# A mixture-of-experts decoder block: down weights by column halves, and a new order of the last steps

## The chip, the cores and the metric

The kernel runs on one core of one Trainium2 chip. The metric is device time in microseconds (us): how long one execution of the whole program takes, weights read from the chip's memory and the result written back to it. The time before is the median of three runs.

## What is computed

The reference is one layer of a decoder for 256 tokens of width 1024 in float32: two kinds of attention side by side, merged by gates (the head of the kernel), then a mixture of 32 experts, and a last norm. The part that the change touches, shortened:

```python
# moe_ffn: each token goes to its 4 best experts of 32, weighted by a softmax
g = xb @ w_gate[e] + b_gate[e]
u = xb @ w_up[e] + b_up[e]
g = jnp.minimum(g, 7.0); u = jnp.clip(u, -7.0, 7.0)
h = (u + 1.0) * g * jax.nn.sigmoid(1.702 * g)
out = h @ w_down[e] + b_down[e]          # summed per token with its gate
x = x + y
return x * rsqrt(mean(x * x, axis=-1) + 1e-5) * norm_final_g   # rms_norm
```

## The kernel before

The experts are worked off two at a time: 16 pairs, each with 64 places for tokens per expert. In `expert_iteration` two pairs make one iteration; the first and the last iteration are written out, the others are a hardware loop. One matmul's left operand holds the 64 tokens of one expert, and the two experts of a pair run side by side in the two halves of the columns of TensorE's array. In float32 one product appears as two matmul instructions in the trace.

The weights of a pair come in 12 loads of 2048 KB (numbers 0 to 3 gate, 4 to 7 up, 8 to 11 down) into a ring of 12 slots that holds just one pair. SyncE (SP) issues them: in the loop two neighbouring loads by one issue (`load_unit`, 4096 KB), in the first and last pairs one by one (`load_half`), and the very last in two pieces (`load_last`). Each issue waits on `load_used`, which TensorE raises when it has done with a slot of the pair before. TensorE waits on `slot_loaded` or `unit_loaded` before it uses one.

The down weights (loads 8 to 11) are laid out by rows: load 8+m holds two of the eight chunks of 128 rows for each of the two experts, over all 1024 columns. `down(w, m, half, c)` adds a chunk's product to one of two accumulator banks, the left 512 columns (`half` 0) or the right. So both halves of the result are complete only when the last load has been used. Between load 8 and load 9 stands `transpose_hidden(1)`, which turns the second half of the hidden layer. When the left half is done (`down_done`) ScalarE copies it to `o_s`, and after the last product the right half (L648). Then TensorE scatters: four products of 512 columns (`scatter(a, half)`, L1486) add the pair's result to `y`, which stays in four accumulator banks over all pairs, one for each block `a` of 128 tokens and each half. In one pair of two, `gather_next` (L1359) then fetches the tokens of the next pair.

After the last pair every engine asks in `rounds_after_first` (L329, L330) whether an expert had more than 64 tokens; it reads one number from memory and branches. Here no second round is run. The end then runs like this. VectorE adds `y` to `x` in four steps of 512 columns (L1068: left and right of block 0, then of block 1). ScalarE loads the table for roots (L654), sums the squares of each step (L658), and takes the root for each block (L663); VectorE prepares a term of it (`half_bias`, L1074) and takes the reciprocal (L1084). Block 0 is multiplied by the norm's weights on GpSimd (L480) and by the reciprocal on ScalarE (L669), block 1 by both on VectorE (L1090). The norm's weights, `gfin`, are read by one load of 512 KB, the same 4 KB for each of 128 partitions, that SP issues when the last pair's hidden layer has been transposed (L443). SP issues the four stores of 256 KB, in the order left and right of block 0, left and right of block 1 (L448), and waits until all have landed.

## Time and profile before

| what | value |
|---|---|
| median of 3 runs | 1138.95 us |
| lowest and highest run | 1138.13 and 1140.11 us |
| the profiled execution's own time | 1142.86 us |
| its span, first to last instruction | 1141.0 us |
| TensorE matmul busy | 1067.4 us, 94% |
| VectorE, ScalarE, GpSimd busy | 210.5, 133.4, 7.9 us |
| mean granted TensorE clock | 0.989 |
| moved by DMA | 438.16 MB, mean 384 GB/s |

The profile is of one execution; its times are counted from the start of the span. "Busy" of TensorE is modelled: matmuls overlap, so one instruction's duration is longer than its share of the time. The granted clock is 1.00 for 2.4 GHz and 0.50 for 1.2 GHz. A row of a timeline names the line of the kernel and the operation, output before input, the count, and in brackets how long the engine stood idle before it and what it waited for. PE is TensorE's matmuls, DVE VectorE, ACT ScalarE; SPq and ACTq are the queues of instructions of SP and ScalarE.

### The profile page before, as it was taken

The numbers are of one execution on the slowest core, as the hardware profiler recorded it, in microseconds if no ns is written. First come the engines' busy times: TensorE is split into PE (matmuls) and PEld (weight loads), VectorE is DVE, ScalarE is ACT, GpSimd is POOL, SyncE is SP. The second block draws the span as 40 slices with busy tenths as digits, with TensorE's granted clock in tenths as the row PEclk, the third lists the DMA queues.
The fourth block names the chain that finished last, engine by engine and source line by source line (L and its number), as shares of the span: only waits on it lengthen the run. The fifth ranks groups of instructions, "written<-read, shape, count | busy, mean of one in ns | idle before, by whom it ended". The sixth has DMA issues, their size and how long they took to land.

```text
span 1141.0 us, 11734 instructions
## 1 busy us (share of the span) xinstructions
PE 1067.4 (94%) x4990; PEld 493.5 (43%) x4990; DVE 210.5 (18%) x508; ACT 133.4 (12%) x227; POOL 7.9 (1%) x17
## 2 busy tenths in 40 slices
PE   8999999989999999999999897989798979998986
PEld 6686888643443434344324332433243324332321
DVE  3132143122211121202020202020202020202021
ACT  1112260111001001000100000001000100010002
POOL 1000000000000000000000000000000000000000
PEclk9999999989999999999999999999999999999998
DMA  9972354589999999999999999999999999999994
GB/s 345 427 304 92 148 219 168 204 345 428 426 434 429 433 430 430 433 431 433 431 432 431 433 430 434 430 434 430 434 430 434 428 435 427 437 421 430 426 428 187
DMA packets 25646, 438.16 MB, mean 384 GB/s; under 512 B 4880, under 2 KB 6160, under 8 KB 8464
## 3 DMA queue, kind: packets, MB, share of 16 engines
q1 hardware_dynamic: 25472, 437.67, 90.5%
q8 instruction: 22, 0.36, 0.1%
q10 hardware_dynamic: 144, 0.07, 0.0%
q14 instruction: 8, 0.07, 0.0%
HBM read 436.28 MB, written 1.05 MB: 383 GB/s over the span
## 4 chain that ended last, share of the span: by engine, by line
PE 70%; DMA 26%; another core or an unknown queue 2%; ACT 1%; DVE 1%; issue 0%; SPq 0%; ACTq 0%; DVEq 0%
PE ps L1433 26%; DMA ring<-in_experts 25%; PE ps L1477 15%; PE ps L1123 9%; PE ps L1359 4%; PE ps L1486 3%; PE ps L1265 2%; PE ps L1114 2%; PE ps L1313 1%; PE ps L1310 1%; PE ps L1142 1%; PE ps L1466 1%; PE ps L1368 1%; ACT region_va L640 1%; PE ps L1378 0%
## 5 line engine op out<-in xcount | busy, mean ns | idle before, releaser
L1433 PE MATMUL ps<-ring,xT 128*64 128x512 f32 x2048 | 453.1, 596 | 28.6 <-DMA ring<-in_experts 28.5
L1433 PEld LDWEIGHTS ps<-ring,xT 128*64 128x64 f32 x2048 | 142.7, 137 | 313.9 <-issue 277.2
L1477 PE MATMUL ps<-ring,region_va 128*64 128x512 f32 x1024 | 233.4, 606 | 28.0 <-DMA ring<-in_experts 18.8
L1477 PEld LDWEIGHTS ps<-ring,region_va 128*64 128x64 f32 x1024 | 73.6, 139 | 166.2 <-issue 129.5
L1123 PE MATMUL ps<-ring 128*128 128x256 f32 x448 | 98.6, 380 | 0.3 <-DVE ring L694 0.3
L1123 PEld LDWEIGHTS ps<-ring 128*128 128x128 f32 x448 | 84.5, 190 | 12.9 <-issue 1.5
L1019 DVE TENSOR_SCALAR g<-ps 128x1024 f32<-128x1024 f32 x16 | 19.6, 1225 | 350.6 <-PE ps L1433 350.6
L1359 PEld LDWEIGHTS ps<-sel,x 128*128 128x128 f32 x480 | 55.4, 192 | 9.5 <-issue 9.5
L1486 PE MATMUL ps<-g,g_T 128*128 128x512 f32 x128 | 59.2, 605 | 0.0
L967 DVE TENSOR_TENSOR xT<-ps,g_ffn 128x512 f32<-128x512 f32 x30 | 20.8, 692 | 197.7 <-PE ps L1359 197.7
L1359 PE MATMUL ps<-sel,x 128*128 128x128 f32 x480 | 56.7, 276 | 0.0
L1041 DVE TENSOR_SCALAR region_va<-ps 128x512 f32<-128x512 f32 x32 | 22.1, 692 | 176.9 <-PE ps L1433 176.9
L634 ACT ACTIVATE region_va<-g 128x1024 f32<-128x1024 f32 x16 | 16.9, 1057 | 318.2 <-DVE g L1019 318.2
L640 ACT COPY region_va<-ps 128x512 f32<-128x512 f32 x32 | 18.8, 586 | 243.6 <-PE ps L1466 243.6
L1486 PEld LDWEIGHTS ps<-g,g_T 128*128 128x128 f32 x128 | 22.9, 189 | 36.0 <-issue 27.5
L648 ACT COPY g<-ps 128x512 f32<-128x512 f32 x32 | 18.8, 587 | 162.6 <-PE ps L1477 162.6
L1114 PE MATMUL ps<-ring 128*128 128x512 f32 x64 | 27.8, 592 | 0.0
L1466 PEld LDWEIGHTS ps<-ident,g 128*128 128x128 f32 x128 | 13.8, 141 | 20.4 <-issue 20.4
L1044 DVE SCALAR_TENSOR_TENSOR g<-region_va,g 128x512 f32<-128x512 f32 x32 | 22.1, 692 | 1.1
L1142 PE MATMUL ps<-ring 128*128 128x256 f32 x64 | 16.4, 420 | 5.0 <-DVE ring L679 5.0
L1466 PE MATMUL ps<-ident,g 128*128 128x128 f32 x128 | 20.3, 281 | 0.0
L1368 PE MATMUL ps<-bias,oh 96*128 96x512 bf16 x64 | 19.7, 389 | 0.0
(200 smaller groups left out, 443.5 us busy)
## 6 DMA issues: line engine op xcount, KB each, us to landing
ring<-in_experts SPq DMA_DIRECT2D x72, 4096.0 KB, 47.5
ring<-in_experts SPq DMA_DIRECT2D x47, 2048.0 KB, 18.4
ring<-in_head SPq DMA_DIRECT2D x13, 2048.0 KB, 16.6
ring<-in_first SPq DMA_DIRECT2D x7, 384.0 KB, 6.1
ring<-in_experts SPq DMA_DIRECT2D x2, 1024.0 KB, 49.5
x<-in_x SPq DMA_DIRECT2D x2, 512.0 KB, 25.0
out<-x SPq DMA_DIRECT2D x4, 256.0 KB, 2.5
ring<-in_norm_final_g SPq DMA_DIRECT2D x1, 512.0 KB, 13.1
```

What stands on the lines that cost most here:

```text
L640: nc.scalar.copy(hTm[:, 4 * b:4 * b + 4, :], bank(second + b).rearrange("p (c s) -> p c s", c=4)).then_inc(hT_ready, 1)
L1041: steps.step(nc.vector.tensor_scalar(u_s[:, cols], bank(second + half), LIMIT, -LIMIT, ALU.min, ALU.max))
L1114: last = mm(bank(b + a), hT[:, c, a * P:(a + 1) * P], w[:, c, :], start=c == 0, stop=c == KC - 1)
L1123: last = mm(bank(b + j // 2)[:, (j % 2) * T:(j % 2 + 1) * T], wj, h, start=c == 0, stop=c == KC - 1)
L1142: last = mm(bank(4 + j)[:, 0:T], w_first[:, c, j * P:(j + 1) * P], hg[:, c, :], start=c == 0, stop=c == KC - 1)
L1265: last = mm(bank(first_bank + j // 2)[:, (j % 2) * T:(j % 2 + 1) * T], w[:, c, j * P:(j + 1) * P], heads[:, c, :], start=c == 0, stop=c == 3)
L1359: last = mm(bank(banks + c // 4)[:, (c % 4) * P:(c % 4 + 1) * P], x3[:, a, c * P:(c + 1) * P], s_sel[:, a, :], start=a == 0, stop=a == NT - 1)
L1368: mm(bank(banks + half), oh[n % 2][0:3 * E, :], bias3[0:3 * E, which, half * W512:(half + 1) * W512], start=True, stop=False, skip_group_c ...
L1433: last = mm(bank(banks + half)[rows, :], xT[:, 2 * m + c, rows], w[:, c, k, half * W512:(half + 1) * W512], start=False, stop=m == 3 and c ...
L1466: last = nc.tensor.transpose(bank(second + b)[:, (c % 4) * P:(c % 4 + 1) * P], g_s[:, c * P:(c + 1) * P], ident)
L1477: last = mm(bank(first + half)[rows, :], hTm[:, 2 * m + c, rows], w[:, c, k, half * W512:(half + 1) * W512], start=m == 0 and c == 0, stop ...
L1486: mm(bank(Y_B + 2 * a + half), g_T[:, a * P:(a + 1) * P], o_s[:, half * W512:(half + 1) * W512], start=False, stop=True, skip_group_check= ...
```

## The change

The down weights are laid out by column halves on the host: loads 8 and 9 hold the left 512 columns of all eight chunks (four chunks each), loads 10 and 11 the right 512 columns. `down(m, chunks)` follows that, and the scatter of the left half (both blocks of tokens) moves between loads 10 and 11; the scatter of the right half stays at the end. ScalarE's copy of the left half waits for load 9's products and that of the right half for load 11's. `transpose_hidden(1)` moves into the middle of load 8. The last load is split at three quarters instead of half.

The norm's weights come at the start as a small load of 4 KB, one column per chunk (`g_fin`). In the last pair TensorE spreads them over all partitions by eight products of 128 columns into two free accumulator banks (`spread_gain`), between loads 9 and 10. The 512 KB load and GpSimd's part are gone. The root table is loaded in the last pair before the left copy. At the end the left halves of both blocks come first: VectorE multiplies them by the norm's weights, ScalarE by the reciprocal; the right halves are multiplied by both on VectorE. SP issues three stores, ScalarE's queue the fourth (left half of block 1). The number of weight bytes, of down products and of scatters is unchanged.

The diff, cut to its core (most removed lines can be seen in the functions above):

```diff
+LAST_COL = 3 * SLOT_COLS // 4
...
-        gfin = whole(SLOT_OF[0])[:, 0:D]
-        xg = whole(SLOT_OF[0])[:, D:2 * D]
+        xg = whole(SLOT_OF[0])[:, 0:D].rearrange("p (a n) -> p a n", a=NT)
...
+        GAIN_B = pair_bank(PAIRS_PER_ITER)
...
+                sp_.dma_start(g_fin[:, :], norm_final_g).then_inc(ld_gfin, 16)
...
-                for c, loaded in enumerate((last_rows, unit_loaded[UNITS - 1])):
-                    cols = slice(c * (SLOT_COLS // 2), (c + 1) * (SLOT_COLS // 2))
-                    from_cols = slice((2 + c) * (SLOT_COLS // 2), (3 + c) * (SLOT_COLS // 2))
-                    sp_.dma_start(whole(SLOT_OF[p])[:, cols], experts_v[row][:, from_cols]).then_inc(loaded, 16)
+                for lo, hi, loaded in ((0, LAST_COL, last_rows), (LAST_COL, SLOT_COLS, unit_loaded[UNITS - 1])):
+                    sp_.dma_start(whole(SLOT_OF[p])[:, lo:hi], experts_v[row][:, SLOT_COLS + lo:SLOT_COLS + hi]
+                                  ).then_inc(loaded, 16)
...
-            rounds = rounds_after_first(sp_, load_iteration)
-            sp_.wait_ge(ht_done, rounds * (2 * PAIRS))
-            sp_.dma_start(gfin, norm_final_g.partition_broadcast(P)).then_inc(ld_gfin, 16)
-            for a in range(NT):
-                for half in range(2):
-                    cols = slice(half * W512, (half + 1) * W512)
-                    sp_.wait_ge((fin_done0, fin_done)[a], half + 1)
-                    sp_.dma_start(out_d[a * P:(a + 1) * P, cols], x3[:, a, cols]).then_inc(stored, 16)
+            rounds_after_first(sp_, load_iteration)
+            for done, a, half in ((fin_right, 0, 1), (fin_left, 0, 0), (fin_right, 1, 1)):
+                cols = slice(half * W512, (half + 1) * W512)
+                sp_.wait_ge(done, a + 1)
+                sp_.dma_start(out_d[a * P:(a + 1) * P, cols], x3[:, a, cols]).then_inc(stored, 16)
...
-            pool.wait_ge(ld_gfin, 16)
-            for half in range(2):
-                cols = slice(half * W512, (half + 1) * W512)
-                pool.wait_ge(y_added, half + 1)
-                nc.gpsimd.tensor_tensor(xg[:, cols], x3[:, 0, cols], gfin[:, cols], ALU.mult).then_inc(fin_g, 1)
...
+            def load_root_table():
+                nc.scalar.activation(table_junk, ones_row[:, 0:2], ACT.Sqrt)
...
+                    if closing and q == PAIRS_PER_ITER - 1:
+                        load_root_table()
                     for b in range(2):
-                        if b == 0:
-                            act.wait_ge(down_done, n + 1)
-                        else:
-                            act.wait_ge(load_used, it * LOADS_PER_ITER + LOADS_PER_PAIR * (q + 2))
+                        act.wait_ge(load_used, it * LOADS_PER_ITER + LOADS_PER_PAIR * (q + 1) + 10 + 2 * b)
                         nc.scalar.copy(o_s[:, b * W512:(b + 1) * W512], bank(first + b)).then_inc(o_ready, 1)
-            with act.Fori(0, ITERS) as i:
+            with act.Fori(0, ITERS - 1) as i:
                 expert_iteration(i, i)
-            rounds_after_first(act, expert_iteration)
-            nc.scalar.activation(table_junk, ones_row[:, 0:2], ACT.Sqrt)
+            expert_iteration(ITERS - 1, ITERS - 1, closing=True)
+            rounds_after_first(act, expert_iteration, closing=load_root_table)
+            def final_squares(a, half):
+                act.wait_ge(y_added, 2 * half + a + 1)
+                nc.scalar.activation(fin_junk[:, (2 * a + half) * W512:(2 * a + half + 1) * W512],
+                                     x3[:, a, half * W512:(half + 1) * W512], ACT.Square,
+                                     accum_out=fin_ssq[:, 2 * a + half:2 * a + half + 1]).then_inc(ssq1_ready, 1)
             for a in range(NT):
-                for half in range(2):
...
+                final_squares(a, 0)
+            for a in range(NT):
+                final_squares(a, 1)
+                act.wait_ge(ssq1_ready, NT + a + 1)
                 act.wait_ge(fin_bias_ready, a + 1)
                 nc.scalar.activation(std[:, a:a + 1], fin_ssq[:, 2 * a + 1:2 * a + 2], ACT.Sqrt, scale=1.0 / D,
                                      bias=fin_bias[:, a:a + 1]).then_inc(fin_std, 1)
...
+            for a in range(NT):
+                act.wait_ge(fin_g, a + 1)
+                act.wait_ge(rstd_ready, a + 1)
+                nc.scalar.activation(x3[:, a, 0:W512], xg[:, a, :], ACT.Copy,
+                                     scale=rstd[:, a:a + 1]).then_inc(fin_left, 1)
+            act.wait_ge(fin_left, NT)
+            act.dma_start(out_d[P:T, 0:W512], x3[:, 1, 0:W512]).then_inc(stored, 16)
...
-                                        resume=lambda: gathered(PAIRS + 1, pair_bank(1)))
...
+                                        resume=lambda: gathered(PAIRS + 1, pair_bank(1)),
+                                        closing=lambda: dve.wait_ge(gain_spread, 4))
+            def add_experts(a, half):
+                cols = slice(half * W512, (half + 1) * W512)
+                dve.wait_ge(sc_done, rounds * (SC_PER_PAIR * PAIRS) + 2 * half + a)
+                nc.vector.tensor_tensor(x3[:, a, cols], bank(Y_B + 2 * a + half), x3[:, a, cols],
+                                        ALU.add).then_inc(y_added, 1)
...
+            def left_gain(a):
+                dve.wait_ge(y_added, a + 1)
+                nc.vector.tensor_tensor(xg[:, a, :], x3[:, a, 0:W512], bank(GAIN_B), ALU.mult).then_inc(fin_g, 1)
+            add_experts(0, 0)
+            add_experts(1, 0)
+            dve.wait_ge(gain_spread, 2)
+            for a in range(NT):
+                left_gain(a)
+            for a in range(NT):
+                half_bias(a)
+            add_experts(0, 1)
+            add_experts(1, 1)
             for a in range(NT):
                 dve.wait_ge(fin_std, a + 1)
                 nc.vector.reciprocal(rstd[:, a:a + 1], std[:, a:a + 1]).then_inc(rstd_ready, 1)
                 dve.wait_ge(rstd_ready, a + 1)
...
+                nc.vector.scalar_tensor_tensor(out=x3[:, a, W512:D], in0=x3[:, a, W512:D], scalar=rstd[:, a:a + 1],
+                                               in1=bank(GAIN_B + 1), op0=ALU.mult, op1=ALU.mult).then_inc(fin_right, 1)
...
+            def spread_gain():
+                pe.wait_ge(ld_gfin, 16)
+                for c in range(KC):
+                    last = mm(bank(GAIN_B + c // 4)[:, (c % 4) * P:(c % 4 + 1) * P],
+                              g_fin[:, c:c + 1].to_broadcast([P, P]), ident, start=True, stop=True)
+                    if c % 4 == 3:
+                        last.then_inc(gain_spread, 1)
...
+                    def down(m, chunks):
+                        s = SLOT_OF[2 * UNITS - 4 + m]
+                        w = whole(s).rearrange("p (c k n) -> p c k n", c=4, k=2)
+                        half, side = divmod(m, 2)
+                        for c in chunks:
+                            for k in range(2):
+                                rows = slice(k * SLOTS, (k + 1) * SLOTS)
+                                last = mm(bank(first + half)[rows, :], hTm[:, 4 * side + c, rows], w[:, c, k, :],
+                                          start=side == 0 and c == 0, stop=side == 1 and c == 3, skip_group_check=True)
                         return last
...
+                    def scatter(half):
+                        pe.wait_ge(o_ready, n * 2 + half + 1)
+                        for a in range(NT):
+                            mm(bank(Y_B + 2 * a + half), g_T[:, a * P:(a + 1) * P],
+                               o_s[:, half * W512:(half + 1) * W512], start=False, stop=True,
+                               skip_group_check=True).then_inc(sc_done, 1)
+                    loaded(8)
+                    pe.wait_ge(hT_ready, n * 2 + 1)
+                    down(0, (0, 1))
+                    transpose_hidden(1)
+                    down(0, (2, 3)).then_inc(load_used, 1)
+                    loaded(9)
+                    pe.wait_ge(hT_ready, n * 2 + 2)
+                    down(1, range(4)).then_inc(load_used, 1)
                     if last_pair:
-                        down(w, 3, 0, 0)
-                        down(w, 3, 1, 0)
+                        spread_gain()
+                    loaded(10)
+                    down(2, range(4)).then_inc(load_used, 1)
+                    scatter(0)
+                    loaded(11)
+                    if last_pair:
+                        down(3, range(3))
                         pe.wait_ge(unit_loaded[UNITS - 1], (n + 1) * 16)
-                        down(w, 3, 0, 1).then_inc(down_done, 1)
-                        down(w, 3, 1, 1).then_inc(load_used, 1)
+                        down(3, (3,)).then_inc(load_used, 1)
                     else:
...
+                        down(3, range(4)).then_inc(load_used, 1)
+                    scatter(1)
...
+            rounds_after_first(pe, expert_iteration, resume=gather_again, closing=spread_gain)
...
-    for w, name in enumerate(("w_gate", "w_up", "w_down")):
+    for w, name in enumerate(("w_gate", "w_up")):
         out[:, w] = a[name].reshape(PAIRS, 2, 2, 4, P, D).transpose(0, 2, 4, 3, 1, 5)
+    by_half = a["w_down"].reshape(PAIRS, 2, KC, P, 2, W512).transpose(0, 4, 3, 2, 1, 5)
+    out[:, 2] = by_half.reshape(PAIRS, 2, P, 4, 2, D)
...
-    give("norm_final_g", a["norm_final_g"])
+    give("norm_final_g", a["norm_final_g"].reshape(KC, P).T)
```

## Rows read from the trace of the kernel before

**Rows 1.** page, the span in 40 equal slices: DMA share in tenths, GB/s
```profile
DMA  9972354589999999999999999999999999999994
GB/s 345 427 304 92 148 219 168 204 345 428 426 434 429 433 430 430 433 431 433 431 432 431 433 430 434 430 434 430 434 430 434 428 435 427 437 421 430 426 428 187
```

**Rows 2.** page, DMA issues: engine, count, KB each, median us to landing
```profile
ring<-in_experts SPq DMA_DIRECT2D x72, 4096.0 KB, 47.5
ring<-in_experts SPq DMA_DIRECT2D x47, 2048.0 KB, 18.4
...
ring<-in_norm_final_g SPq DMA_DIRECT2D x1, 512.0 KB, 13.1
```

**Rows 3.** windows: us, busy (x) per engine, clock, DMA share, GB/s
```profile
504.33:556.88 52.55, 51.78 (x247) 19.95 (x247) 8.85 (x19) 5.06 (x7) 0.00 (x0) 1.00 1.00 430
```

**Rows 4.** chain of waits, 1110 to 1141 us: start, us, what
```profile
1120.96 8.81 PE ps L1477 x32
...
1129.94 0.48 ACTq L329
```

**Rows 5.** timeline of TensorE, 1094 to 1132 us: start, us, line, operation
```profile
1104.58 3.65 PE L1433 MATMUL ps<-ring,xT 128*64 128x512 f32 x16 [1.24 <-DMA ring<-in_experts]
...
1114.36 3.65 PE L1477 MATMUL ps<-ring,region_va 128*64 128x512 f32 x16 [0.53 <-DMA ring<-in_experts]
1120.96 8.78 PE L1477 MATMUL ps<-ring,region_va 128*64 128x512 f32 x32 [2.95 <-DMA ring<-in_experts]
1129.68 2.84 PE L1486 MATMUL ps<-g,g_T 128*128 128x512 f32 x6
```

**Rows 6.** windows of the low clock (columns as in rows 3)
```profile
1122.00:1125.00 3.00, 3.00 (x10) 0.75 (x8) 0.00 (x0) 0.00 (x0) 0.00 (x0) 0.51 0.27 112
```

**Rows 7.** issues of loads 9 and 10, then of load 11, landings; queues 1118 to 1119
```profile
L393 SPq DMA_DIRECT2D ring<-in_experts x2: 434/2343/4252, 1063.0 to 1067.3; - x2
...
DMA to landing us min/median/max: 51.3/52.5/53.6
...
L407 SPq DMA_DIRECT2D ring<-in_experts x2: 4249/7905/11561, 1069.1 to 1080.7; - x2
...
DMA to landing us min/median/max: 45.0/49.5/54.1
...
q8 instruction: 1, 0.02, 6.9%
```

**Rows 8.** timeline of ScalarE, 1110 to 1141 us
```profile
1113.87 0.59 ACT L640 COPY region_va<-ps 128x512 f32<-128x512 f32 x1 [4.42 <-PE ps L1466]
...
1130.89 1.28 ACT L654 ACT_TABLE_LOAD   x1 [0.51 <-issue]
...
1132.29 0.61 ACT L658 ACTIVATE region_va<-x 128x512 bf16<-128x512 f32 x1
...
1135.22 0.29 ACT L663 ACTIVATE small<-small 128x1 f32<-128x1 f32 x1
1135.42 1.32 ACT L669 ACTIVATE x<-ring,small 128x512 f32<-128x512 f32 x2
```

**Rows 9.** timeline of VectorE, 1128 to 1141 us
```profile
1130.84 0.69 DVE L1068 TENSOR_TENSOR x<-ps,x 128x512 f32<-128x512 f32 x1 [21.14 <-PE ps L1486]
...
1135.98 0.16 DVE L1084 RECIPROCAL small<-small 128x1 f32<-128x1 f32 x1 [1.13 <-ACT small L663]
1136.18 1.42 DVE L1090 SCALAR_TENSOR_TENSOR x<-x,small,ring 128x512 f32<-128x512 f32 x2
```

**Rows 10.** issues of the stores on SP; the load on ScalarE's queue with its landing
```profile
L448 SPq DMA_DIRECT2D out<-x x4: 348/439/777, 1136.2 to 1138.1; - x4
...
ident<-in_const ACTq DMA_DIRECT2D x1, 64.0 KB, 4.0
```

**Rows 11.** timeline of TensorE, whole pairs in the middle
```profile
542.37 10.52 PE L1477 MATMUL ps<-ring,region_va 128*64 128x512 f32 x48
...
646.18 3.84 PE L1359 MATMUL ps<-sel,x 128*128 128x128 f32 x32
```

76 lines of the change are left out of this document (10 added, 66 removed).

## Prediction

> **What bounds the kernel now.** I read the page's slices first [rows 1]: from the tenth slice (of 28.5 us each) to the last but one the DMA engines are full and move about 430 GB/s. The issue table [rows 2] gives the expert weights: 72 x 4096 + 47 x 2048 KB and the last slot in two halves of 1024, together 402.7 MB, so 25.17 MB for each of the 16 pairs of experts. At 430 GB/s one pair takes 58.5 us. A pair whose TensorE never waits takes 52.55 us [rows 3] (the window between equal points of two neighbouring pairs, 51.78 us of it busy). The middle of the kernel is therefore bound by the weight stream, with about 6 us of TensorE slack in each pair, and only what stands behind the last weights can move the end.
>
> So I followed the chain of waits [rows 4] and TensorE's timeline [rows 5] over the last 25 us. The last pair's down weights come in four loads, 8 to 11. Load 9 is multiplied from 1114.36 to 1118.0; then TensorE stands still for 2.9 us until load 10 lands at 1120.9, runs the 32 matmul instructions of loads 10 and 11 in 8.81 us to 1129.77, and goes on with the four scatters. From there the chain is ScalarE's: copy of the right half, the check for more rounds, a table load of 1.28 us, squares, roots, then VectorE's last two products and the stores [rows 8 to 10]. From 1129.77 to the end of the span, 1141.0, are 11.23 us.
>
> Two oddities in this stretch are accidents of timing that the change meets. First, the granted clock falls to 0.5 (1.2 GHz) after the standstill: the window 1122 to 1125 shows a mean of 0.51 [rows 6], TensorE having done nothing from 1118.0 to 1120.9. The 32 instructions at full clock would take 3.65 us for 16 [rows 5] and 3.43 us for each further 16 (10.52 less 3.65, halved [rows 11]), so 7.1 us; the low clock cost 1.7 us. Second, load 10 is late: load 9 was issued at 1063.0 and took 51.3 us, load 10 at 1067.3 and 53.6 us [rows 7]: landings at 1114.3 and 1120.9, 6.6 us apart for 2048 KB, where the rate gives 4.9 us. In between, a packet of 16 KB on the instruction queue took 6.9% of 16 engines for 1 us, so 1.1 us of one engine [rows 7].
>
> **The change, part by part.** TensorE's end. Before, all four 512-column scatters stand behind load 11. After, loads 8 and 9 hold the left half of the down weights and 10 and 11 the right, so the left half is complete at 1118.0 and ScalarE, idle since 1114.5 [rows 8], copies it then. While TensorE waits for load 10 it spreads the norm's weights: 8 products of 128 columns, 16 instructions. The nearest rows are the gather's 32 instructions in 3.84 us [rows 11], so 1.9 us. It lies in the 2.9 us of standstill and costs nothing; without that cover it would cost 1.9. Then come load 10 (16 instructions, 3.43), the two left scatters (4 instructions, 6 take 2.84 with 0.17 of drain, so 1.78 for 4 [rows 5]), load 11 (3.43) and 0.17 of drain: 8.8 us. At full clock the last down product ends at 1120.96 + 8.8 = 1129.8, exactly where it ends now: the left scatters have taken the place of the clock loss. I take full clock, because only 1.0 us of standstill is left, and a stop of 1.24 us in this stretch is followed by full speed (3.65 us for 16 instructions [rows 5]). If the clock falls all the same, add 1.7 us.
>
> Load 11's pieces are now 1536 and 512 KB instead of twice 1024. They landed at 1123.2 and 1125.7 (1069.1 + 54.1, 1080.7 + 45.0; the longer time is the first one's [rows 7]); the first moves to about 1124.5, the second stays. TensorE asks for them at 1126.2 and 1128.8: hidden, by 1.7 and 3.1 us. The 512 KB load of the norm's weights goes away. It is issued behind load 11 on the same queue, after the hidden layer's second transposes (ended by 1113.9), and lands 13.1 us later [rows 2], 1.2 us behind the last weights, so I give it nothing; had it gone between the weights, 1.2 us (512 KB at 430 GB/s) would be won. In its place comes one small load among the start's. The nearest issues hold SP for 0.35 to 0.78 us [rows 10], ahead of most of the head's weights; there the DMA engines soon fall to two to five tenths [rows 1], the head is not short of weights, so again nothing, and 0.8 us at worst.
>
> ScalarE's and VectorE's end, counted from t = the last down product. Unchanged: the copy of the right half starts at 0.03 and takes 0.59, and the round check keeps ScalarE until 1.12 (1129.77 to 1130.89 [rows 4, 8]). The table load of 1.28 and its small activation (1130.89 to 1132.29 together, 1.40 us) have moved into ScalarE's idle time before the left copy (1114.5 to 1118.0, cover 3.5 us). Squares of the left half, 0.61 each: 1.12 to 1.73 and to 2.34, the last sum read out at 2.45. VectorE's two small half_bias steps wait for these sums, and the adds of the right half are queued behind them: this is the new wait. The scatter could release the first add at 0.66 + 1.16 = 1.82 (copy end to first scatter to first add, 1129.68 to 1130.84 [rows 5, 9]), but half_bias holds it to 2.65. Adds: to 3.35 and 3.98. First right square 3.42 to 4.03, sum read to 4.12, root 4.15, second square from 4.36, read to 5.06, root 5.10 to 5.39 (steps and distances as in ScalarE's timeline now, where the second root runs 1135.22 to 1135.51 [rows 8]). From the root's start to the reciprocal are 0.76 us (1135.22 to 1135.98 [rows 8, 9]): reciprocals at 4.91 and 5.88, products of one 512-column half each, 0.75, at 5.11 and 6.08, the last to 6.83. ScalarE's two left products (1.32 for two [rows 8]) end at about 6.8 too, and the copy waits for the same reciprocal.
>
> The Trainium skill (ScalarE: Activation LUTs, section What ACT_TABLE_LOAD costs) gives 1283 ns for the load, as the row does, but adds about 1380 ns of drain for every switch of tables, 2.66 us in all. The rows show the first square 0.12 us behind the load's end, and before the load only 0.5 us without an instruction [rows 8]. By the page the removed switch would give back 2.66 us instead of my 1.40, an estimate of 1136.4 us for the median instead of the sum below; rival 4 is the part of it for which the rows leave room.
>
> Stores. Now the fourth of four on SP starts at 1138.1, although VectorE is done at 1137.6, because each keeps SP for 0.35 to 0.78 us, and its landing ends the span, 2.9 us after that start [rows 10]. After, the third on SP and the one on ScalarE's queue both start at about 6.9. With 2.9 us behind them the span ends at t + 9.8, against 11.23 now: 1.4 us less. Two stores of 256 KB landing together add at most 0.6 us (256 KB at 430 GB/s); I take 0.1. The only load on ScalarE's queue took 4.0 us to land [rows 10], 1.1 more than those 2.9: the upper bound.
>
> Each pair in the middle. The scatter of the right half must now wait for its copy: the last product, 0.03 + 0.59 + about 0.1. That is 0.7 to 0.8 us of TensorE standstill a pair where there was none (the first scatter starts as the products end, 1129.68 [rows 5]). It lies in the 6 us of slack. The slots of loads 10 and 11 come free 1.8 us later than now; the stream's queue covers that (the 2048 KB loads, most of them at the stream's start and its end, land 18.4 us after their issue in the median, over 13 of that behind others [rows 2]).
>
> **Sum.** Span 1141.0 + 0.0 (TensorE) - 1.4 + 0.1 (the tail) = 1139.7; with the 1.9 us around it (1142.86 - 1141.0) 1141.6. The median of the runs, 1138.95, lies 3.9 us under the profiled run, so I apply the difference, -1.3 us: 1137.7.
>
> **The rivals.**
> 1. The clock falls in spite of the spread products: +1.7 - 1.3 = +0.4, 1139.4. For it: a standstill of about 1 us is left. Against: the stop of 1.24 us without a fall. The Trainium skill (TensorE: Matmul & The Clock Gate, section Part 1) has the throttled state as the default, released by activity; by that the spread products can help and not harm.
> 2. Load 10 is on time in ordinary runs, which would also explain why these are 3.9 us shorter than the profiled one (1.6 us of lateness and 1.7 us of clock). Then before restarts at 1119.3 and ends its products at 1126.4; after can't start load 10 before the spread ends (1118.0 + 1.9 = 1119.9, then 8.8: 1128.7). TensorE loses 2.3, the tail gives 1.3: +1.0, 1140.0.
> 3. Load 10 is late before and on time after, because the instruction packet falls elsewhere: TensorE ends at 1128.7 instead of 1129.8, together -2.4: 1136.5.
> 4. The tail gives more: if ScalarE's 0.5 us between its last copy and the next instruction [rows 8] belongs to the table load and not to the round check, the squares start 0.5 us earlier; with stores landing a little sooner 2.0 to 2.5 in all: 1136.7.
> 5. Slower: the new wait in each pair makes TensorE the bound. 15 pairs x 0.75 = 11 us if no slack were left, 1149. It decides only once a pair needs more than 58.5 us; 52.55 + 0.75 = 53.3 speaks against it. A part of it is possible at the start of the stream, where the queue is thin.
> 6. The change does not do what it says at the tail: the store on ScalarE's queue lands 1.1 us later and eats most of the gain: -0.2, 1138.8.
>
> **How the numbers follow.** Chances: forecast 0.42, rival 1 0.10, rival 2 0.20, rival 3 0.10, rival 4 0.07, rival 5 0.05, rival 6 0.06. A measurement of this kernel can tell 0.2%, 2.3 us, from no change. Faster by more takes rival 3, part of 4 and the quick edge of the forecast: 0.22. Slower by more takes rival 5 and the slow edges of 1 and 2: 0.12. Within: 0.66. The range goes from rival 3 less 0.6 us of the runs' own spread, 1135.9, to rival 2 plus the same, 1140.6; the likeliest case alone reaches from 1136.6 to 1138.9.
>
> **What would show it.** In the profile after: 16 gain instructions in about 1.9 us right after load 9; no window under full clock behind 1120; the left scatter between loads 10 and 11; the last down product within 0.3 us of 1129.8; no table load behind the last copy; the first right add at about t + 2.7, after the second half_bias; the last store issued near t + 6.9; the span 9.8 to 10.0 us behind t. In the middle the DMA share stays at 1.00 and each pair shows a stop of 0.7 us before its right scatter. The prediction is wrong if load 10 lands at another time, if the clock falls, or if the DMA share sinks anywhere between 250 and 1110 us.

## The result and the profile after

The changed kernel takes 1142.87 us (median of 15 runs, 1141.35 to 1144.84), the kernel before, beside it, 1139.65 us (15 runs, 1138.13 to 1142.17). The ratio is 1.0028, with a 95% interval of 1.002 to 1.0035: 3.2 us slower. A second measurement (e10, below) gave 1142.92 against 1139.79. The forecast was 1137.7 us and the range ended at 1140.6.

The profiled run of the change has a span of 1141.1 us, that of before had 1141.0 us. They look equal, and that is the first thing to see: every run here takes 1.7 to 2.0 us more than its span, so the profiled run of before took 1142.86 us, 3.2 above its own median, and that of the change 1142.87 us, its median.

TensorE's end after the change, from its timeline (start, us, line, operation, [idle before <- what ended it]), to be laid beside [rows 5]:

```profile
1113.20 1.94 PE L1500 MATMUL ps<-ring,region_va 128*64 128x512 f32 x8
1115.51 3.65 PE L1500 MATMUL ps<-ring,region_va 128*64 128x512 f32 x16 [0.38 <-DMA ring<-in_experts]
1119.10 2.05 PE L1410 MATMUL ps<-ident,g_fin 128*128 128x128 f32 x16
1121.08 3.65 PE L1500 MATMUL ps<-ring,region_va 128*64 128x512 f32 x16
1124.66 1.98 PE L1508 MATMUL ps<-g,g_T 128*128 128x512 f32 x4
1126.58 3.65 PE L1500 MATMUL ps<-ring,region_va 128*64 128x512 f32 x16
1130.92 1.98 PE L1508 MATMUL ps<-g,g_T 128*128 128x512 f32 x4 [0.69 <-ACT g L646]
```

Each piece lies where the prediction put it: the spread products (L1410) behind load 9, the left scatter (the first L1508) between loads 10 and 11, and the stop of 0.69 us in which the right scatter waits for ScalarE's copy. But from 1115.51 on TensorE has no wait for a load any more. The standstill of 2.95 us of [rows 5] is gone, and with it every cover: load 10 had landed at 1120.3 (issued at 1064.3, 56.0 us to landing, in the rows of the issues below), and TensorE began it at 1121.08.

```profile
L398 SPq DMA_DIRECT2D ring<-in_experts x5: 432/4242/11586, 1049.6 to 1064.3; - x5
...
DMA to landing us min/median/max: 51.2/52.4/56.0
```

ScalarE's and VectorE's end, the timelines that answer to [rows 8, 9]; the last down product ends at t = 1130.26 and its copy starts 0.02 us later:

```profile
1130.28 0.58 ACT L646 COPY g<-ps 128x512 f32<-128x512 f32 x1 [10.48 <-PE ps L1500]
1131.55 0.63 ACT L656 ACTIVATE region_va<-x 128x512 bf16<-128x512 f32 x1 [0.69 <-issue]
...
1133.74 0.63 ACT L656 ACTIVATE region_va<-x 128x512 bf16<-128x512 f32 x1 [0.86 <-DVE x L1072]
...
1135.63 1.32 ACT L671 ACTIVATE x<-ring,small 128x512 f32<-128x512 f32 x2
1136.98 0.36 ACTq L674 DMA_DIRECT2D out<-x  x1
```
```profile
1132.91 0.15 DVE L1078 TENSOR_SCALAR small<-small 128x1 f32<-128x1 f32 x1 [0.46 <-ACT region_va L656]
1133.01 1.29 DVE L1072 TENSOR_TENSOR x<-ps,x 128x512 f32<-128x512 f32 x2
...
1135.96 0.75 DVE L1099 SCALAR_TENSOR_TENSOR x<-x,small,ps 128x512 f32<-128x512 f32 x1
```

The table load is gone from here, the second half_bias (L1078) holds the right adds to t + 2.75 (forecast 2.65), VectorE's last product ends at t + 6.45 (forecast 6.83). Up to here the tail is as forecast or better. Yet from t to the end of the span are 10.8 us, not 9.8. The rest is stores. SyncE's three issues (line, engine, start and length on its queue) from its timeline:

```profile
1135.80 2.41 SPq L449 DMA_DIRECT2D out<-x  x3
```

The second of them alone takes 1.33 us (from 1136.37), so the third starts at t + 7.5 and not at t + 6.9.

The middle, in the page's 40 slices (GB/s), against [rows 1]:

```profile
GB/s 346 426 301 95 148 210 168 212 331 430 412 436 434 429 431 431 431 433 430 434 430 434 428 435 427 436 427 436 427 436 426 438 426 438 425 428 429 427 428 191
```

The ninth slice (228 to 257 us), in which the stream begins, shows 331 where before has 345; SyncE's run of 12 issues begins 0.9 us later in this profile (243.08 against 242.15), and 0.9 us at 430 GB/s are those 14. The eleventh (285 to 314 us) shows 412 where before has 426. It is the first slice within the stream in which the changed kernel moves clearly less; e10 to e12 below go into it.

### The profile page after: what moved, and what is told of

Read it like the earlier page. It is cut to its first block, busy times and chain, and to the rows that moved or that the text cites. A ratio compares the mean times of both kernels' runs of the same rounds, so it can differ in the third digit from the quotient of the medians.

```text
span 1141.1 us, 11751 instructions
## 1 busy us (share of the span) xinstructions
PE 1076.3 (94%) x5006; PEld 492.2 (43%) x5006; DVE 211.8 (19%) x510; ACT 132.2 (12%) x226; POOL 5.3 (0%) x15
## 3 DMA queue, kind: packets, MB, share of 16 engines
HBM read 435.76 MB, written 1.05 MB: 383 GB/s over the span
## 4 chain that ended last, share of the span: by engine, by line
PE 70%; DMA 26%; ACT 1%; DVE 1%; issue 1%; another core or an unknown queue 1%; SPq 0%; ACTq 0%; DVEq 0%
PE ps L1451 28%; DMA ring<-in_experts 26%; PE ps L1500 13%; PE ps L1132 9%; PE ps L1508 3%; PE ps L1368 3%; PE ps L1274 2%; PE ps L1123 2%; PE ps L1322 1%; PE ps L1319 1%; PE ps L1151 1%; PE ps L1484 1%; PE ps L1377 1%; ACT region_va L639 1%; ACT g L646 1%
## 5 line engine op out<-in xcount | busy, mean ns | idle before, releaser
L1500 PE MATMUL ps<-ring,region_va 128*64 128x512 f32 x1024 | 233.0, 599 | 18.8 <-ACT region_va L639 11.5
L1500 PEld LDWEIGHTS ps<-ring,region_va 128*64 128x64 f32 x1024 | 70.1, 137 | 156.7 <-issue 131.0
L1508 PE MATMUL ps<-g,g_T 128*128 128x512 f32 x128 | 63.5, 618 | 11.0 <-ACT g L646 11.0
L1508 PEld LDWEIGHTS ps<-g,g_T 128*128 128x128 f32 x128 | 21.7, 189 | 53.4 <-issue 28.3
L1484 PEld LDWEIGHTS ps<-ident,g 128*128 128x128 f32 x128 | 14.1, 143 | 21.2 <-issue 21.2
```

What stands on the lines that cost most here:

```text
L1484: last = nc.tensor.transpose(bank(second + b)[:, (c % 4) * P:(c % 4 + 1) * P], g_s[:, c * P:(c + 1) * P], ident)
L1500: last = mm(bank(first + half)[rows, :], hTm[:, 4 * side + c, rows], w[:, c, k, :], start=side == 0 and c == 0, stop=side == 1 and c == 3, ...
L1508: mm(bank(Y_B + 2 * a + half), g_T[:, a * P:(a + 1) * P], o_s[:, half * W512:(half + 1) * W512], start=False, stop=True, skip_group_check= ...
```

## The experiments

An interval of a ratio here is about 0.1% to either side, 1.1 us, so a step of one experiment beside another is known to about that; the profiles tell more exactly where a microsecond lies. All differences are given against the runs of the kernel before in the same set.

**e1: is it the place of the left scatter?**

```diff
                     down(2, range(4)).then_inc(load_used, 1)
-                    scatter(0)
+                    if not last_pair:
+                        scatter(0)
...
                         down(3, (3,)).then_inc(load_used, 1)
+                        scatter(0)
```

> The changed kernel, but in the last pair the left scatter stands behind the products of load 11 again (two scatters of the left half, then two of the right). Theory A (the loss of 3.2 us is TensorE work that used to lie behind or beside other work and now stands between the landing of load 10 and the last scatter): the last product ends 1.9 us sooner, the wait of 0.69 us for the copy of the right half is covered by the left scatter, VectorE's adds start 0.6 to 0.7 us sooner, so the time falls by 0.6 to 0.7 us against the changed kernel, to about 2.5 us over the kernel before. Theory B (the weight stream starts or runs later since the head of the kernel, and the end only follows it): no difference from the changed kernel beyond 0.3 us.

1141.97 us, ratio 1.0012 (1.0003 to 1.0021): of the 3.2 us 1.4 are gone. TensorE's timeline:

```profile
1119.70 2.05 PE L1410 MATMUL ps<-ident,g_fin 128*128 128x128 f32 x16
1122.44 7.30 PE L1500 MATMUL ps<-ring,region_va 128*64 128x512 f32 x32 [0.69 <-DMA ring<-in_experts]
1129.67 3.70 PE L1508 MATMUL ps<-g,g_T 128*128 128x512 f32 x8
```

The products of loads 10 and 11 are one piece again, and the scatters lie behind the last of them, where ScalarE's copy and round check run beside them. The 0.69 us shown here isn't the copy's stop, which is gone; it is a wait for load 10, whose products begin 6.3 us behind load 9's in this execution, nearly as late as in the profiled run of before (6.6), and not 5.6. So the column "to t" in the table below (13.7 us) holds 0.7 us that the edit didn't cause. Theory A expected 0.6 to 0.7 us and got 1.4: it let only the start of the adds count. From load 10's start on, t comes 1.8 us sooner than in the changed kernel, and the tail is 0.3 us longer (11.1 against 10.8), which leaves about 1.5 us, an estimate from these two profiles.

**e2: is it the spread products?** The norm's weights come by the 512 KB load as before, and TensorE doesn't spread them.

```diff
-                    if last_pair:
-                        spread_gain()
...
+            sp_.dma_start(gfin, norm_final_g.partition_broadcast(P)).then_inc(ld_gfin, 16)
```

> The changed kernel, but the norm's weights come by the 512 KB load of the kernel before and TensorE spreads nothing. Theory A: load 10 lands 4.9 us behind load 9 and TensorE starts it on landing, 0.8 us sooner than now (1120.3 instead of 1121.1), and the end moves by the same 0.8, if the granted clock stays full; a fall of the clock would cost up to 1.7 us and eat it. Theory B: no difference beyond 0.3 us.

1142.76 us, ratio 1.0021 (1.0012 to 1.003). The products of load 10 began at 1121.76, 4.9 us behind those of load 9 and on its landing (a wait of 1.23 us), against 5.57 us in the changed kernel. The spread products cost 0.7 us of their 2.0. The median is 0.6 us nearer to the kernel before than the changed kernel's (2.6 against 3.2 us), in line with it, but within the noise.

**e3: is it the stores?** All four go out from SyncE's queue.

```diff
-            for done, a, half in ((fin_right, 0, 1), (fin_left, 0, 0), (fin_right, 1, 1)):
+            for done, a, half in ((fin_right, 0, 1), (fin_left, 0, 0), (fin_right, 1, 1), (fin_left, 1, 0)):
...
-            act.dma_start(out_d[P:T, 0:W512], x3[:, 1, 0:W512]).then_inc(stored, 16)
```

> The changed kernel with all four stores issued by SP (right and left of block 0, right and left of block 1). If two queues that issue at the same time hold each other up (SP's second issue took 1.33 us beside ScalarE's, the longest before was 0.78), the last store starts no later than now (1137.7) and the time is the same within 0.3 us or shorter by up to 0.5. If the second queue saves what it seems to, the fourth issue comes 0.4 to 0.5 us later and the time rises by that.

1143.54 us, ratio 1.0031 (1.0019 to 1.0043), not to be told from the changed kernel. SyncE's second issue takes 1.34 us here too, with no store on ScalarE's queue: that the two queues hold each other up is ruled out as its cause. The profile holds something else: here load 10 was late, as in the profiled run of before.

```profile
1114.15 3.65 PE L1498 MATMUL ps<-ring,region_va 128*64 128x512 f32 x16 [0.39 <-DMA ring<-in_experts]
1117.74 2.05 PE L1408 MATMUL ps<-ident,g_fin 128*128 128x128 f32 x16
1120.43 3.65 PE L1498 MATMUL ps<-ring,region_va 128*64 128x512 f32 x16 [0.64 <-DMA ring<-in_experts]
```

From load 9's products to t are 15.5 us, against 15.4 in [rows 5], with no low clock. In this case, nearly the one that I forecast (load 10's products begin 6.3 us behind load 9's, and not 6.6), the change costs next to nothing at TensorE's end.

**e4: is it the small load at the start?** The kernel before with one more load of 4 KB.

```diff
+                sp_.dma_start(g_fin[:, :], norm_ffn_g).then_inc(ld_gfin, 16)
...
-            pool.wait_ge(ld_gfin, 16)
+            pool.wait_ge(ld_gfin, 32)
```

> The kernel before with one extra small load of 4 KB among the small loads of the start, at the place where the changed kernel has it (its waits on the old load count both). Theory B, in the form that the extra issue of 0.44 to 0.49 us delays the head's weights and with them the whole stream: 0.5 to 1.2 us slower than before. Theory A: the same within 0.3 us.

1139.77 us, ratio 0.9997 (0.9988 to 1.0006): it isn't. Its profiled run took 1141.97 us, 2.2 above its median, and shows load 10 late again and the 32 products in 8.78 us.

**e5: the kernel before, once more.**

> The kernel before once more, for a second profile. Theory A' (the profiled execution of before that the prediction was worked from is one of its slow ones: load 10 late by 1.6 us, then the low clock): if this one's time is near the median of 1140, load 10 is started about 4.9 us after load 9, the 32 products of loads 10 and 11 take 7.3 us instead of 8.8, and the span ends 23 to 24 us after the start of load 9's products, against 26.6 in that profile and 25.6 in the changed kernel's. If it is one of the slow ones, 26 to 27 us again. Rival: the end takes 26 us in typical executions too, and the lower median comes from the head or the middle: then load 9's products start 2 to 3 us sooner than at 1114.4.

1139.66 us, ratio 0.9998 (0.9988 to 1.0008); the profiled run took 1139.7, so this is an ordinary one:

```profile
1114.40 3.65 PE L1477 MATMUL ps<-ring,region_va 128*64 128x512 f32 x16 [0.53 <-DMA ring<-in_experts]
1119.31 5.37 PE L1477 MATMUL ps<-ring,region_va 128*64 128x512 f32 x24 [1.25 <-DMA ring<-in_experts]
1124.86 1.94 PE L1477 MATMUL ps<-ring,region_va 128*64 128x512 f32 x8 [0.18 <-DMA ring<-in_experts]
1126.73 3.70 PE L1486 MATMUL ps<-g,g_T 128*128 128x512 f32 x8
```

Load 9's products begin where they do in [rows 5] (1114.40 against 1114.36), but load 10's 4.9 us later and not 6.6, and the 32 instructions take 7.3 us with the full clock, besides a wait of 0.18. The last down product ends at 1126.8, 3.0 us earlier. Only 10 of the 117 runs of the kernel before that were measured beside the others took over 1141.5 us; the two profiled runs with load 10 late took 1142.9 and 1142.0. That fits load 10 being late in few runs, though only a profile shows it.

**e6: TensorE's part alone**, on the kernel before: the weights by halves, the left scatter between loads 10 and 11, the pieces of three and one quarters, and the copies' waits; tail, stores and the norm's load as before.

```diff
-                        if b == 0:
-                            act.wait_ge(down_done, n + 1)
-                        else:
-                            act.wait_ge(load_used, it * LOADS_PER_ITER + LOADS_PER_PAIR * (q + 2))
+                        act.wait_ge(load_used, it * LOADS_PER_ITER + LOADS_PER_PAIR * (q + 1) + 10 + 2 * b)
...
+                    down(2, range(4)).then_inc(load_used, 1)
+                    scatter(0)
```

> The kernel before with the down weights by column halves, the left scatter between loads 10 and 11, the copies' waits and the split of the last load as in the changed kernel; the end (table load behind the last copy, norm's weights by the 512 KB load, GpSimd's part, four stores on SP) as before. Theory A (TensorE's order): the last product comes 1.9 us later by the left scatter, ScalarE's copy and chain with it, so 1.6 to 1.9 us slower than before in median. Rival (the loss sits in the new end, the two queues or the order of the adds): the same as before within 0.5 us.

1142.21 us, ratio 1.0025 (1.0015 to 1.0035): 2.3 us slower, more than the 1.6 to 1.9 expected. Most of the loss of 3.2 us is in this part. Its profile has t 1.7 us further behind load 9's products than e5, and load 9's products begin 2.4 us further behind the start of the loads.

**e7: both undone at the end**, the edits of e1 and e2 together.

> The changed kernel with both edits of the first two experiments: left scatter of the last pair behind load 11, norm's weights by the 512 KB load, no products for them. Theory A: TensorE's part is that of before again in the last pair; against the changed kernel 1.2 (measured with the scatter alone, 0.0012 against 0.0028) plus up to 0.8 us, so about 0.6 us over the kernel before, within 0 to 1.2. If the waits for the copy in the middle pairs cost anything, it stays above 1.2.

1140.90 us, ratio 1.001 (1.0001 to 1.0019). It lies within the expected 0 to 1.2. From load 9's products to t are 12.8 us, 0.3 more than in e5 (TensorE waits 0.5 us for load 11's first piece), and the tail has 0.1 more. So at most half of the 1.0 us that remains is at the end.

**e8: the left scatters behind load 11 in all pairs**, on top of e7; in the tail GpSimd does the left products, and VectorE's order is add, add, half_bias, add, half_bias, add.

```diff
-                    down(2, range(4)).then_inc(load_used, 1)
-                    scatter(0)
...
                         down(3, range(4)).then_inc(load_used, 1)
+                    scatter(0)
                     scatter(1)
```

> As the one with late scatter and load, but in every pair both scatters of the left half stand behind load 11; GpSimd multiplies the left halves by the norm's weights (1.27 us each, beside VectorE's adds), and VectorE does add, add, half_bias, add, half_bias, add. Last root at t + 5.25, last product of VectorE until t + 6.85 instead of t + 7.83 in the kernel before, last store issued near t + 7.2: 0.6 to 1.0 us faster than before by theory A. If the end is worth nothing, or VectorE and GpSimd slow each other by 0.5 us or more, the same as before within 0.5 us.

1140.06 us, ratio 1.0 (0.9991 to 1.0009): level with the kernel before, with the weights by halves and a new order of the tail still in it. The 0.6 to 1.0 us that theory A expected did not come; the rival did, an end that is worth nothing, although VectorE is done at t + 6.5 and not at t + 7.8. Against e7, in the same set, it is 0.8 us faster; 0.5 of that can be e7's wait for load 11.

**e9: the root's table early, alone**, on the kernel before.

```diff
+                    if closing and q == PAIRS_PER_ITER - 1:
+                        load_root_table()
...
-            nc.scalar.activation(table_junk, ones_row[:, 0:2], ACT.Sqrt)
```

> The kernel before with one edit: ScalarE loads the root's table after the last copy of the hidden values, and not behind the second copy of the down product. If the table load sets when the squares can begin (in e5_before_again it ran from 1127.94 to 1129.2, behind 0.51 us of issue, and the first sum that the squares need is ready at about 1128.7), about 0.5 us is gained (ratio 0.9996); if the sums of VectorE set it anyway, nothing. Either way the tail of the kernel before can't be what e8_all_behind leaves to win.

1139.45 us, ratio 0.9995 (0.9984 to 1.0005), nothing that could be told. In its profile the first square begins at t + 1.8 instead of t + 2.5, on an add of VectorE, and the last product ends 0.3 us earlier, counted from t.

**e10: the changed kernel, once more.**

> The changed kernel unchanged, a second time: its profile shows whether load 10 is on time there too (the products of load 9 begun, and 4.9 us later those of load 10, with the spread products inside), whether the wait of 0.7 us for the right copy and the slow second issue on SyncE (1.33 us) come again, and whether its products of load 9 begin about 1 us later than in the kernel before (1114.4 in three profiles of it). Time about 1142.8.

1142.92 us, ratio 1.0024 (1.0014 to 1.0033). Again 5.57 us from load 9's products to load 10's, and 14.8 to t; the stop of 0.69 us is there too, and SyncE's slow second issue (1.52 us). Load 9's products begin at 1116.68, even later. What delays them shows in SyncE's issues and in the windows of the profiles. The 12 issues of loads that begin at 243 us take 44.83 us in the kernel before (e5, first line) and 46.89 here (second fence):

```profile
242.96 44.83 SPq L393 DMA_DIRECT2D ring<-in_experts  x12
302.29 653.20 SPq L398 DMA_DIRECT2D ring<-in_experts  x72
```
```profile
242.90 46.89 SPq L398 DMA_DIRECT2D ring<-in_experts  x12
303.33 656.06 SPq L403 DMA_DIRECT2D ring<-in_experts  x72
```

The windows 290 to 300, 300 to 310 and 310 to 330 us (the last two figures are the DMA share and GB/s), e5 first, then e10:

```profile
290.00:300.00 10.00, 10.00 (x61) 5.82 (x61) 1.38 (x2) 0.00 (x0) 0.00 (x0) 1.00 1.00 424
300.00:310.00 10.00, 10.00 (x48) 3.16 (x46) 1.02 (x1) 0.00 (x0) 0.00 (x0) 1.00 1.03 431
310.00:330.00 20.00, 19.23 (x108) 8.91 (x106) 7.47 (x18) 2.02 (x3) 0.00 (x0) 1.00 1.01 433
```
```profile
290.00:300.00 10.00, 9.89 (x58) 5.93 (x60) 1.38 (x2) 0.05 (x1) 0.00 (x0) 1.00 1.01 427
300.00:310.00 10.00, 10.00 (x49) 3.19 (x46) 0.00 (x0) 0.00 (x0) 0.00 (x0) 1.00 0.97 385
310.00:330.00 20.00, 19.23 (x106) 8.82 (x108) 8.50 (x18) 2.01 (x3) 0.00 (x0) 1.00 1.02 437
```

What SyncE waits for between 243 and 290 us, in all, times and longest, in e5 and then in the changed kernel (L1477 and L1500 are the down products):

```profile
SPq L393 <- PE ps L1477: 14.7, 4, 4.7
```
```profile
SPq L398 <- PE ps L1500: 16.8, 4, 5.4
```

In the first pairs TensorE is busy nearly throughout and SyncE waits for it to give slots back. The left scatter, 1.98 us, stands ahead of load 11's release (load 10's slot is released before it); SyncE waits 2.1 us longer for the down products, and in 300 to 310 us the transfers fall to 374 to 401 GB/s in the seven profiles with this order in the first pairs, against 413 to 431 in the seven without (with those of e11 and e12 below). The last two experiments test this, each on the changed kernel.

**e11: the left scatters behind load 11 in every pair but the last.**

```diff
-                    scatter(0)
+                    if last_pair:
+                        scatter(0)
...
+                    if not last_pair:
+                        scatter(0)
                     scatter(1)
```

> The changed kernel, its left scatters behind load 11 in every pair but the last. New theory: besides the end, the new order costs the stream of loads about 1.1 us once, near 300 us: there TensorE has no waits, so that the left scatter (1.98 us) before load 11, and the wait of 0.69 for the right copy, give back the slots later, SyncE's 12 issues from 243 take 46.9 us and not 44.8, and the DMAs move 374 to 387 GB/s in 300 to 310 us, against 416 to 431. Then these 12 issues take 44.8 again, 300 to 310 us shows about 430 GB/s, load 9's products begin near 1114.5, and the time is about 1141.8 (1.1 below the changed kernel, ratio 1.0017). The rival, that the stream isn't touched (what a single profile shows there is chance): 1142.8.

1142.09 us, ratio 1.0021 (1.0012 to 1.003). The 12 issues are back to what they were, and the window nearly:

```profile
243.30 44.83 SPq L398 DMA_DIRECT2D ring<-in_experts  x12
302.63 653.26 SPq L403 DMA_DIRECT2D ring<-in_experts  x72
```
```profile
300.00:310.00 10.00, 10.00 (x48) 3.18 (x46) 0.67 (x1) 0.00 (x0) 0.00 (x0) 1.00 1.01 419
```

The time fell by 0.8 us against the changed kernel (2.3 above before instead of 3.1), less than 1.1 but on its side; the runs alone don't prove it. What is left, 2.3 us, is the size of what the end costs by the profiles (see below).

**e12: in the first two pairs alone** (`if not opening`, `if opening` in the same places).

> The same, but in the first two pairs alone. If what is lost is lost once, where TensorE is what the loads wait for, this gives back as much as e11_loops_left_late: 1141.8. If each pair costs the stream a little: 1142.7, and e11_loops_left_late is faster than this one.

1142.73 us, ratio 1.0024 (1.0015 to 1.0034). The start is mended (44.84 us), yet the 72 issues then took 656.75 us (653.26 in e11), and the gain is 0.2 us. That speaks against "lost once" and for a part in the loops' later pairs. But it is one profile, and the 0.6 us between the medians of e12 and e11 are within the noise: it isn't settled.

All together, in us. First: how long the 12 issues take; then from their start to load 9's products; from those to t (the copy's start in ScalarE's timeline); from t to the end of the span; and the median against before.

| | 12 issues | to load 9 | to t | tail | median |
|---|---|---|---|---|---|
| before, profiled (load 10 late) | 44.8 | 872.2 | 15.4 | 11.2 | |
| e4 small load (load 10 late) | 44.8 | 871.4 | 15.2 | 10.9 | -0.4 |
| e5 before again | 44.8 | 871.4 | 12.4 | 11.0 | -0.3 |
| e9 table early | 44.8 | 871.6 | 12.5 | 11.0 | -0.3 |
| e8 all behind | 44.8 | 871.9 | 12.3 | 10.9 | +0.2 |
| e11 loops' left late | 44.8 | 871.7 | 14.8 | 10.6 | +2.3 |
| e12 opening's left late | 44.8 | 872.3 | 14.8 | 11.5 | +2.9 |
| after | 46.9 | 872.4 | 14.8 | 10.8 | +3.2 |
| e10 after again | 46.9 | 873.8 | 14.8 | 11.0 | +3.1 |
| e1 scatter late (load 10 late) | 46.9 | 872.9 | 13.7 | 11.1 | +1.8 |
| e2 gain by load | 46.9 | 874.0 | 14.1 | 10.8 | +2.6 |
| e3 one queue (load 10 late) | 46.9 | 871.5 | 15.5 | 10.9 | +3.4 |
| e6 TensorE's part | 46.9 | 873.8 | 14.1 | 11.2 | +2.3 |
| e7 e1 and e2 | 46.9 | 873.3 | 12.8 | 11.1 | +1.0 |

## Why the prediction was wrong

**What was right.** The order and the length of TensorE's pieces, the copy's stop of 0.69 us in each pair (forecast 0.7 to 0.8), load 11's landings (issued 1076.0 and 1080.2, landed 1124.5 and 1125.7; forecast 1124.5 and 1125.7), no fall of the clock behind the spread products, the table load hidden, the half_bias as the new wait, and VectorE's last product within 0.4 us. For an execution in which load 10 is late the forecast of TensorE's end held to 0.1 us, 15.5 us in e3 against 15.4, and part of that is luck: load 10's products began 0.3 us sooner than forecast, and from there to t were 9.2 us, not 8.8. The 8.8 took 3.43 us for each 16 down instructions and 1.78 for the scatter; each change between them adds about 0.15 (starts at 1121.08, 1124.66 and 1126.58).

**The step that failed first** is the one from one execution to the median: "The median of the runs, 1138.95, lies 3.9 us under the profiled run, so I apply the difference". The difference was worked out in an execution with load 10 late and 1.5 us of low clock (8.78 us for the 32 instructions against 7.30 in e1; the prediction has 1.7), and those are just what makes that execution longer than its median. Of the four profiles of kernels with the old end, two have it (before, e4: 1142.9 and 1142.0 us) and two don't (e5, e9: 1139.7 both). In the ordinary case TensorE waits 1.25 us for load 10, keeps its clock, and reaches t 12.4 us behind load 9's products. There the change adds 5.57 - 4.91 = 0.66 us of uncovered spread products and the 1.9 us of the left scatter, and saves the 0.2 us that the second piece of load 11 was waited for: 14.8 us, 2.3 more. That is rival 2, with its term of TensorE as written (2.3), and I had it at 0.20; its sum, 1140.0, still fell short, since it counted on the tail's 1.3 us and took nothing for the stream. e2 takes the spread products away (14.1 in the column "to t"), e1 the left scatter (13.7, of which 0.7 is its late load 10), e7 both (12.8, with 0.5 of a wait for load 11).

The left scatter was cheap before: behind the last product the scatters run beside ScalarE's round check and table load (to 1129.2 in e5, 2.4 us behind t), and the adds take one bank after the other. Moved ahead of load 11's products, all of it counts. I had priced what the move adds there, and not that it takes almost nothing away behind t.

**The second, "the stream's queue covers that"**, fell too. I weighed the slots' later release in the middle of the stream, where DMA is full, and not at its start, where TensorE is what the loads wait for. (Only load 11's slot comes free later, not load 10's as the prediction has it.) The text named the place (rival 5: "at the start of the stream, where the queue is thin") and gave it no price. In the column "to load 9" the six profiles with the left scatters behind load 11 outside the last pair have 871.4 to 872.2, mean 871.7; the seven with them ahead 871.5 to 874.0, mean 873.1 (e12, with both orders, 872.3). That they are later, by 1.4 us on average, is shown by these and by the 12 issues; how it is passed on through the loops isn't settled, and the two groups overlap (e3 has 871.5).

**The third is the tail's 1.3 us** (1.4 less 0.1). From t to the end of the span are 10.6 to 11.5 us in the variants of the changed kernel, against 11.0 in e5: nothing is gained, though VectorE is done at t + 6.4 and not at t + 7.8. Two terms failed. The first is the start of SyncE's last issue, forecast at t + 6.9 and measured at t + 7.5. The stores do start earlier (t + 5.5 against t + 6.4 in e5), but the second issue took 1.33 us. It took 1.09 to 2.04 us in each of the seven profiles whose first store is issued at t + 5.5 to t + 5.6 (after, e2, e3, e8, e10, e11, e12), and 0.34 to 0.88 in the seven others. The second term is what stands behind the last issue: 3.4 us to the end of the span, where the kernel before has 2.9; each store landed 2.9 to 3.1 us after its issue, in e5 2.3 to 2.5. (The prediction took all of the 2.9 for the landing; there the last store landed 2.5 us after its issue.)

A packet of 16 KB on the instruction queue q8 goes with the slow issue. Here the second issue after the change and the packet between 1136.0 and 1136.2 us, 0.2 to 0.4 us behind the start of the first issue (its row gives packets, MB and the share of 16 engines in that window):

```profile
1136.37 1.33 SPq L449 DMA_DIRECT2D out<-x  x1
```
```profile
q8 instruction: 1, 0.02, 38.3%
```

And in e1, where the packet falls between 1135.4 and 1135.6 us, 0.8 to 1.0 us ahead of the first issue:

```profile
1136.96 0.34 SPq L449 DMA_DIRECT2D out<-x  x1
```
```profile
q8 instruction: 1, 0.02, 32.6%
```

Over all 14 profiles: a packet 0.2 to 0.6 us behind the first issue's start goes with a second issue of 1.09 to 2.04 us (seven), one from 0.3 us ahead to level with it with 0.78 to 0.88 us (before, e6, e9), one 0.8 to 0.9 us ahead with 0.34 to 0.55 us (e1, e4, e5, e7). No run moves this packet by itself, so it isn't shown to be the cause, which stays open.

The slices of the DMA windows show how the data flowed: the changed kernel in slices of 0.275 us from 1134, then e5 in slices of 0.25 us from 1130.

```profile
DMA  0000000203982099999995000000000000000000
GB/s 30 0 0 0 0 0 0 60 0 134 357 343 75 15 372 380 373 387 402 380 380 201 15 0 0 0 0 0 0 0 0 0 0 0 0 0 0 0 0 0
```
```profile
DMA  0000010002000010799699999998000000000000
GB/s 0 0 0 0 0 33 0 0 0 66 0 0 0 0 33 0 287 369 336 221 377 401 361 418 352 377 393 303 0 0 0 0 0 0 0 0 0 0 0 0
```

The result is 1.05 MB, and at these 380 GB/s it needs 2.8 us. In e5 it flows from t + 7.2 to t + 10.2 with hardly a gap. After the change it flows from t + 6.2, stops for 0.5 us while SyncE is in its second issue, and ends at t + 10.0; the span ends 0.8 us later in both. Without the stop the span would have ended near t + 10.3, an estimate: so the shared rate takes a part of the gain and the slow issue another. A second queue brought nothing that could be told (e3). The earlier table, a part of the 1.4, gives 0.3 us by itself (e9), because the adds are next in line.

**The other rivals.** Rival 1 fell: behind the spread products the granted clock is 1.00 in all six profiles that have them (1118 to 1133 us). Rival 3 needs an execution of before with load 10 late as the usual one, and it isn't. Rival 4 fell: with the table load hidden, 0.69 us without an instruction still stand between ScalarE's copy and its first square, so they aren't the table load's. The round check's last row ends at 1131.11, 0.25 us behind the copy; what the other 0.44 us are isn't shown. The Trainium skill (ScalarE: Activation LUTs, section What ACT_TABLE_LOAD costs) adds about 1380 ns of drain to a switch. The traces here don't show it: in e5 ScalarE stands 0.51 us before the load of 1.28 us and 0.01 us behind it, and in e9 the load begins 0.03 us behind the copy ahead of it. How much a hidden switch gives back, e9 can't tell, as its first square waits for an add. Rival 5 as written (TensorE becomes the bound) fell, since the DMA share stays at 1.00 from 500 to 1000 us. Rival 6 fell as written: the store from ScalarE's queue landed 3.1 us after its issue, the others 2.9 to 3.1; but all landed later than the 2.3 to 2.5 us of e5.

The whole, for ordinary runs: 2.3 us at the end and about 1.4 in the stream, nothing from the tail, 3.7 against 3.2 measured (with an interval of 2.3 to 4.0).

## What to carry to other kernels

Compare the profiled execution's own time with the median before summing on it. If it lies above, look for a late transfer or a low clock in the very stretch that you cost, and make the sum for an execution without it: a cover that exists only where a transfer is late hides nothing in the others. Work that is moved ahead of a release delays the transfers in the stretch where the engine, and not the memory, is the bound, even if the middle has slack; read the thin part of the stream by itself. And before earlier stores are credited, ask two things: how long each issue holds its queue, and how long the bytes of all the stores need at the rate at which the last ones flow.

## What the runs showed of the hardware

- Load 10's products began 4.9 us after load 9's in one execution (e5) and 6.6 in another ([rows 5]) of the same program, with load 9's at the same time (1114.4); e1, e3 and e4 show 6.3. The packet on the instruction queue that stood in the late one [rows 7] is at 1118 in e5 as well, where load 10 is on time; so it isn't the cause by itself, and what is stays open.
- A standstill of TensorE of 2.68 and 2.95 us in this place was followed by 1.2 GHz (8.78 us for 32 instructions, e4 and [rows 5]); one of 1.23 to 1.25 us was followed by full clock each time (e2, e5, e6, e7, e8, e9).
- Three issues of 256 KB stores kept SyncE's queue 1.40 us (e1, e7) to 3.10 us (e12) from the first to the end of the last, in nearly the same code. The second of them took 0.34 to 2.04 us, and it took over 1 us exactly in the seven profiles in which a 16 KB instruction packet fell 0.2 to 0.6 us behind the first issue's start.
